# Two-block model on one core: shared modulation sums, index keys first, diagonal norms

## What is computed

```python
# first block
ada = c @ w_ada + b_ada                        # [1024] @ [1024, 6144]
shift1, scale1, gate1, shift2, scale2, gate2 = split(ada, 6)
h = rms_norm(x, g_norm1) * (1 + scale1) + shift1
zq, zk, zv, ziq, zik, ziw, zp, zg = split(h @ w_in)
q = rms_norm(zq by head, g_q); k = rms_norm(zk, g_k); ik = rms_norm(zik, g_ik)
# every query takes the 64 keys with the best index score:
#   sum over 4 index heads of relu(iq . ik) * iw, then softmax attention over them
y_attn = attention(q, k, zv, chosen) @ w_up_attn
y_pool = pool_mixer(zp) @ w_up_pool
g_attn, g_pool = split(sigmoid(zg))
x = x + gate1 * ((g_attn * y_attn + g_pool * y_pool) @ w_out)
h2 = rms_norm(x, g_norm2) * (1 + scale2) + shift2
x = x + gate2 * peer_ffn(h2)                   # 16384 experts, 8 heads, top 16
# second block: rms_norm, recurrent branch, sparse attention, w_out, rms_norm, gated FFN
```

## Time and profile before

| | |
|---|---|
| median of three runs | 1694.33 us |
| profiled execution, its own time | 1695.2 us |
| its span, first to last instruction | 1693.4 us |
| TensorE busy | 1560.6 us, 92% |
| VectorE, ScalarE, GpSimd busy | 1108.9, 841.4, 1102.9 us |
| mean granted TensorE clock | 0.968 of full speed |
| DMA | 280.07 MB, mean 165 GB/s |

### The profile page before, as it was taken

How to read it: one execution, slowest core, us unless ns; L and a number is a source line. 1 busy time by engine, 2 the same in 40 slices (tenths; PEclk the granted TensorE clock), 3 DMA queues, 4 the chain that set the end, 5 groups by cost and what they waited for, 6 DMA issues and landing times. The chain is left out here.

```text
span 1693.4 us, 27007 instructions
## 1 busy us (share of the span) xinstructions
PE 1560.6 (92%) x9679; PEld 1367.5 (81%) x9679; DVE 1108.9 (65%) x1674; ACT 841.4 (50%) x1432; POOL 1102.9 (65%) x453
## 2 busy tenths in 40 slices
PE   1789868999999999999999999999999988799999
PEld 1666536999999999988888888798877756699987
DVE  6555456799937777768888888761645364268760
ACT  1443304555556666645545454547654364454442
POOL 0663004688986666658888888856883622578896
PEclk9989889999999999999999999999999989999999
DMA  7645365455454444435555555535543511445554
GB/s 264 234 141 186 116 222 182 162 186 174 166 172 149 148 138 138 140 120 190 197 188 196 191 193 195 197 113 198 199 162 127 159 51 38 137 159 179 185 186 138
DMA packets 77397, 280.07 MB, mean 165 GB/s; under 512 B 8577, under 2 KB 9089, under 8 KB 77186
## 3 DMA queue, kind: packets, MB, share of 16 engines
q1 hardware_dynamic: 76592, 276.68, 48.3%
q10 hardware_dynamic: 722, 2.27, 0.4%
HBM read 277.86 MB, written 1.05 MB: 165 GB/s over the span
## 5 line engine op out<-in xcount | busy, mean ns | idle before, releaser
L1977 POOL TENSOR_TENSOR low<-ring,high 128x1024 fp32r<-128x1024 f32 x449 | 1102.6, 2468 | 579.9 <-ACT high L945 579.7
L945 ACT ACTIVATE high<-ring 128x1024 fp32r<-128x1024 f32 x449 | 472.2, 1057 | 419.6 <-PE PS L346 400.2
L344 PE MATMUL PS<-hTh,high 128*128 128x256 f32 (+1 forms) x1648 | 472.4, 287 | 7.3 <-POOL low L1977 6.1
L346 PE MATMUL PS<-hTh,low 128*128 128x256 f32 (+1 forms) x1648 | 467.7, 284 | 0.0
L345 PE MATMUL PS<-hTl,high 128*128 128x256 f32 (+1 forms) x1648 | 467.5, 284 | 0.0
L344 PE MATMUL PS<-high,hTh 128*128 128x512 f32 x940 | 371.9, 396 | 15.8 <-POOL low L1977 10.9
L345 PE MATMUL PS<-low,hTh 128*128 128x512 f32 x940 | 368.5, 392 | 0.0
L346 PE MATMUL PS<-high,hTl 128*128 128x512 f32 x940 | 368.4, 392 | 0.0
L1725 DVE TENSOR_TENSOR hTl<-region,hTh 128x256 fp32r<-128x256 f32 x128 | 289.1, 2260 | 59.8 <-ACT hTh L1177 59.8
L344 PEld LDWEIGHTS PS<-hTh,high 128*128 128x128 f32 (+1 forms) x1648 | 317.6, 193 | 10.2 <-POOL low L1977 5.4
L345 PEld LDWEIGHTS PS<-hTl,high 128*128 128x128 f32 (+1 forms) x1648 | 317.1, 192 | 0.0
(11 more groups left out here) (287 smaller groups left out, 1568.5 us busy)
## 6 DMA issues: line engine op xcount, KB each, us to landing
ring<-in_stream SPq DMA_DIRECT2D x523, 512.0 KB, 3.3
X<-in_x SPq DMA_DIRECT2D x1, 1024.0 KB, 5.0
region<-in_band ACTq DMA_DIRECT2D x1, 1024.0 KB
result<-X SPq DMA_DIRECT2D x4, 256.0 KB, 2.0
region<-in_skeys ACTq DMA_DIRECT2D x1, 512.0 KB
region<-in_consts ACTq DMA_DIRECT2D x1, 352.0 KB, 3.8
region<-in_wpool ACTq DMA_DIRECT2D x1, 256.0 KB
cols<-in_cols SPq DMA_DIRECT2D x1, 208.0 KB, 5.0
```

Of the source, the lines that this page charges most:

```text
L344: pe.matmul(out_, sh, mh, start=start, stop=False, **kw)
L346: return pe.matmul(out_, sl, mh, start=False, stop=stop, **kw)
L945: act.activation(high[:, b % RING, :], ring[:, b % RING, :], ACT.Copy).then_inc(rounded[b % RING], 1)
L1977: pool.tensor_tensor(low[:, b % RING, :], ring[:, b % RING, :], high[:, b % RING, :].bitcast(F32), ALU.subtract).then_inc(left[b % RING], 1)
```

## The change

1. **Modulation blocks 0 to 3 are shared.** TensorE multiplies quarters 0 and 2 itself (`ada_product`), into one row of PSUM, which ScalarE copies to `ada_row`; VectorE keeps quarters 1 and 3. The closing sums on TensorE are then four matmuls of the row and four with `ones`.
2. **n1's transposes come ahead of the modulation sums**, and ScalarE rounds two quarters of in0 before it splits n1. Five loads (band, wpool, brow, skeys, iota) are issued by ScalarE after the index keys and not before n1's split; lambda's work moves behind the attention.
3. **Index keys first.** Their squares, sum, root and scaling are done alone; TensorE transposes the index queries straight from `Z`, then the keys (six transposes) between in2 and in3. Queries and keys are scaled during in3 and transposed (ten) between the pooling products and in6, behind the copies of the pooling.
4. **Blocks 9 and 4** leave their places: `ada9` and `ada4` stand ahead of up_attn in the stream, and VectorE does one quarter of them in each of the eight steps of the attention loop. Sums 6 to 9 follow m1's transposes.
5. **up_attn and out1 finish bank by bank** (`bank_done`), VectorE gates each bank as it is done, and m1's first eight transposes start after three of them. Sums 4 and 5 stand after out1's second quarter instead of its third.
6. **Norms by a diagonal.** Rows are no longer scaled: VectorE writes diag(1/rms) for both token tiles, and the transpose becomes a float32 matmul of `X` with it. The root takes scale and bias itself.

```diff
-PAIRED = {"in1": "ada6", "in6": "ada7", "up_pool": "ada8", "up_attn": "ada9", "out0": "ada5", "out1": "ada10",
+PAIRED = {"in1": "ada6", "in6": "ada7", "up_pool": "ada8", "out0": "ada5", "out1": "ada10",
...
-    for name in [...] + ["up_pool", "up_attn", "ada4", "out0", "out1", "pq0", "pq1"]:
+    for name in [...] + ["up_pool", "ada9", "ada4", "up_attn", "out0", "out1", "pq0", "pq1"]:
...
+        ADA_ON_PE = (0, 2)
...
 # TensorE
-            def transposes(tag, src, ready, n_ready):
-                pe.wait_ge(sem(ready), n_ready)
+            def transposes(tag, src, ready, n_ready, by=None, first_half=None):
+                pe.wait_ge(sem(ready), first_half or n_ready)
                 for c in range(KC):
+                    if first_half and c == KC // 2:
+                        pe.wait_ge(sem(ready), n_ready)
                     for t in range(T):
...
+                        if by is None:
+                            last = pe.transpose(dst, part, ident[:, :])
+                        else:
+                            last = pe.matmul(dst, part, by[:, t, :], start=True, stop=True)
...
+                    if j < 4:
+                        for q in range(4):
+                            pe.matmul(PS[:, 7, 4 * j + q:4 * j + q + 1], ada_row[0:1, j, q * P:(q + 1) * P],
+                                      ones[0:1, 0:1], start=(q == 0), stop=False, skip_group_check=True)
+                        wait_used(pe, f"ada{j}")
...
+            def ada_product(j, q):
+                wait_loaded(pe, f"ada{j}", q)
+                for c in range(2):
+                    last = pe.matmul(PS[0:1, 5 + j % 2, :], col("cT", 2 * q + c), slot(f"ada{j}", q)[:, c, :],
+                                     start=(q == ADA_ON_PE[0] and c == 0), stop=(q == ADA_ON_PE[-1] and c == 1))
+                free_slot(f"ada{j}", q, last)
...
-            for j in range(4):
-                wait_used(pe, f"ada{j}")
-                ada(j)
-            transposes("n1", XN1, "norm_scaled", nth_norm("n1", T, T))
+            transposes("n1", X, "norm_scaled", nth_norm("n1", T, T), by=diag)
+            for j in range(5):
+                for q in ADA_ON_PE:
+                    if j < 4:
+                        if j >= 2 and q == ADA_ON_PE[0]:
+                            pe.wait_ge(sem("ada_row_kept"), j - 1)
+                        ada_product(j, q)
+                    if j and q == ADA_ON_PE[0]:
+                        pe.wait_ge(sem("ada_row_kept"), j)
+                        ada(j - 1)
...
-            transposes("qk1", N1, "qk1_normed", 1)
+            turned1(5, Z)
+            turned1(6, Z)
+            pe.wait_ge(sem("ik1_normed"), 1)
+            turned1(7, N1).then_inc(sem("ik1_turned"), 1)
             z1(3)
-            pe.wait_ge(sem("turned_kept"), kept_by("qk1", KC))
+            pe.wait_ge(sem("ik1_kept"), 2)
...
+            pe.wait_ge(sem("pool_kept"), 4)
+            pe.wait_ge(sem("qk1_normed"), 1)
+            for c in range(5):
+                last = turned1(c, N1)
+            last.then_inc(sem("qk1_turned"), 1)
             z1(6)
...
-            for j in (6, 7, 8):
-                wait_used(pe, f"ada{j}")
-                ada(j)
             attention("a1")
             pe.wait_ge(sem("attn1_kept"), 2)
+            token_major("up_attn", OT1, lambda t, o: 4 + 2 * t + o, per=1, inner=D, bank_done="up_done")
+            transposes("m1", M1, "m1_ready", 4, first_half=3)
+            for j in (6, 7, 8, 9):
+                wait_used(pe, f"ada{j}")
+                ada(j)
...
-            out1(0, 1, 2)
+            out1(0, 1)
             for j in (4, 5):
...
-            out1(3)
-            transposes("n2", XN1, "norm_scaled", nth_norm("n2", T, T))
+            out1(2, 3, done="out1_done")
+            transposes("n2", X, "norm_scaled", nth_norm("n2", T, T), by=diag)
...
 # VectorE
+                link(dve.reciprocal(tiny[:, 6:6 + T], tiny[:, 4:4 + T]))
+                for t in range(T):
+                    dve.tensor_tensor(diag[:, t, :], ident[:, :], tiny[:, 6 + t:7 + t].broadcast_to([P, P]),
+                                      ALU.mult).then_inc(sem("norm_scaled"), 1)
...
+                    if tag == "a1" and u < n:
+                        ada((9, 4)[u // QUARTERS], [u % QUARTERS])
...
+            normed1_heads(slice(9, 10), 1, [(896, IK1, 9, 1, 2)], "ik1_normed")
...
+            normed1_heads(slice(0, 9), 3, [(0, 0, 0, H1, 1), (512, K1, H1, 1, 2)], "qk1_normed")
...
-            ada(9)
-            ada(4)
-            wait_used(dve, "up_attn")
...
+                        dve.wait_ge(sem("up_done"), 2 * t + half + 1)
```

More of the change, by code:

```diff
@@ L94, in plan @@
     order = [f"ada{j}" for j in range(4)]
-    for name in [f"in{i}" for i in range(Z1B)] + ["up_pool", "up_attn", "ada4", "out0", "out1", "pq0", "pq1"]:
+    for name in [f"in{i}" for i in range(Z1B)] + ["up_pool", "ada9", "ada4", "up_attn", "out0", "out1", "pq0", "pq1"]:
         order += [name] + [PAIRED[n] for n in [name] if n in PAIRED]
@@ L666, in _, with out1 @@
             pe.wait_ge(sem("y_pool_kept"), 4)
[L667 removed]
+            pe.wait_ge(sem("qk1_kept"), 3)
+            attention("a1")
+            pe.wait_ge(sem("attn1_kept"), 2)
+            token_major("up_attn", OT1, lambda t, o: 4 + 2 * t + o, per=1, inner=D, bank_done="up_done")
+            transposes("m1", M1, "m1_ready", 4, first_half=3)
+            for j in (6, 7, 8, 9):
                 wait_used(pe, f"ada{j}")
                 ada(j)
[L670 to L676 removed]
             pe.wait_ge(sem("turned_kept"), kept_by("m1", KC))
+            def out1(*quarters, done=None):
+                token_major("out1", MT1, lambda t, o: 5 + 2 * t, quarters=quarters, bank_done=done)
+            token_major("out0", MT1, lambda t, o: 4 + 2 * t)
             pe.wait_ge(sem("ada_kept"), 2)
[L680 to L684 removed]
+            out1(0, 1)
             for j in (4, 5):
@@ L791, in _ @@
                         last.then_inc(sem("v_done"), 1)
[L794 removed]
+            transposes("n3", X, "norm_scaled", nth_norm("n3", T, T), by=diag)
             for i in range(RT_N):
@@ L1552, in _, with normed1_heads @@
-            dve.memset(m8[:, :], 0.0).then_inc(sem("qk1_normed"), 1)
-            keep_turned("qk1", NT1, lambda c: col("gain1", c))
+            def normed1_heads(heads, root, parts, done):
+                by_token = [st1[:, i, :].rearrange("p (t h) -> p t h", t=T)[:, :, heads] for i in range(3)]
+                dve.wait_ge(sem("qk1_root"), root)
+                link(dve.reciprocal(by_token[0], by_token[1]))
+                for t in range(T):
+                    for dst, src, h, n, dup in parts:
+                        weight = bc(st1[:, 0, 10 * t + h:10 * t + h + n], 2, HD)
+                        value = Z[:, t, src:src + n * HD].rearrange("p (h d) -> p h d", h=n)
+                        ins = dve.tensor_tensor(N1[:, t, dst:dst + dup * n * HD].rearrange("p (h d) -> p h d", h=dup * n),
+                                                value if dup == 1 else value.broadcast_to([P, dup, HD]),
+                                                weight if dup == 1 else weight.broadcast_to([P, dup, HD]), ALU.mult)
+                ins.then_inc(sem(done), 1)
@@ L1613, in _ @@
             for half in range(2):
-                wait_used(dve, f"out{half}")
                 for t in range(T):
+                    if half and not t:
+                        dve.wait_ge(sem("out1_done"), 1)
+                    else:
+                        wait_used(dve, f"out{half}")
                     o = half * NB
```

182 lines of the change are left out of this document (98 added, 84 removed).

## The result

The changed kernel takes 1678.31 us (median of three runs, 1677.88 to 1681.22) against 1694.33: a ratio of 0.9912, 95% interval 0.9889 to 0.9934. The profiled execution has a span of 1676.1 us against 1693.4, 17.3 less. Two later sets of runs of the same file, each beside the kernel before on the same chip, gave 1682.13 against 1696.37 and 1680.97 against 1697.80, a ratio of 0.9892 (0.9842 to 0.9943) and 0.9908 (0.9880 to 0.9935), with spans of 1684.2 and 1681.4.

What follows compares the result with a forecast made beforehand. TensorE was taken as the bound, busy 1560.6 of 1693.4 us, its idle 133 us nearly all there was to win. Terms summed to -13.0: 1695.2 to 1682.2, or 1681 against the median; range 1669 to 1692.

Steps and rivals of the forecast that it cites:

- Index keys first: Block 2 to block 3 of the projection: nearly all of TensorE's wait and slow transposes go, -10.3 us.
- rival 2: GpSimd's passes hold the new VectorE operations; index keys, then scoring, come 5 us late: 1686 us; chance 0.14.
- The ten other transposes: Behind the pooling copies: TensorE waits for ScalarE's four copies, 2.1 us, and transposes, 1.1: +3.2 us.
- Start: From the start to projection block 2: sums gain little, the first product follows them sooner; -6.5 us, bounds -9 and +8.
- Attention: Attention loop: eight modulation quarters added to VectorE only partly fit its idle time; +8.8 us with 1 for the clock.
- rival 4: Attention loop: the added quarters fill all of VectorE's idle time, +4 us instead of +8.8, total 1676; chance 0.12.
- up_attn to out0: Between these two products: sums gone from the path, gates bank by bank; -8.5 us after allowing for low clock.
- The end of out1: t=0's bank ends 3.4 us early and out0's gates no longer wait for gate1: -1.4 us.
- the prediction's last sentence: Wrong if the peer stage starts within 3 us of the old start, or a new wait behind it takes the gain.
- Norms by a diagonal: Three norms on the path: 16 more records each outweigh the scaling saved; +4.1 us, between 0 and +8.5.
- Rival 3: Diagonal for nothing: true matmuls lift the clock early, so the norms' price goes, 4.1 us less, 1677; chance 0.15.
- Rival 1: Low clock, slower: half clock stays in the four modulation blocks and the attention loop, total 1699 us; chance 0.09.

Runs made afterwards that it cites:

- c0: The changed kernel again, unchanged, timed beside the kernel before: 1682.13 us against 1696.37, ratio 0.9892.
- c1: The changed kernel once more, unchanged, timed beside the kernel before: 1680.97 us against 1697.80, ratio 0.9908.
- The two experiments on it: Each on the changed kernel: n2's squares ahead of ScalarE's roundings, 1677.48 us; out1's last two quarters not bank by bank, 1677.96 us.
- both orders: Changed kernel with block 0's products before n1's transposes, n2's squares before the roundings, and an earlier table load: 1665.54 us, later 1664.30.

## Why the prediction was right, and where it was not

The forecast of 1681 was 2.7 us above the result, and the two later medians, 1682.13 and 1680.97, lie within 1.2 us of it. The mechanism was right for the index keys, the ten transposes, the sums before attention and up_attn; the closeness of the sum is in part luck, as errors of 3 to 7 us in three terms cancelled. The steps:

- **Index keys first** came as worked out: no wait before block 3, transposes at full clock (0.82 us), -9.7 to -11.3 against -10.3. (The -9.7 of the first profile holds a fall of the clock inside block 2, 0.50 granted from 79.1 to 82.5; the other two have none there.) The two multiplies were held, 3.65 us together, but were done at 86.1, 4.5 us before TensorE came, so rival 2 fell:

```profile
82.49 3.65 DVE L1596 TENSOR_TENSOR region<-region 128x128 f32<-128x128 f32 x2
```

- **The ten other transposes** measured +3.1 for +3.2, 1.66 of it the wait for ScalarE's copies; **the sums before attention** -3.0 for -2.9. **Block 3** gave -0.9 for +0.5: scoring held nothing back, and the slow products that the forecast had counted with the index keys lay here, at 0.50 granted to 104.7 before.
- **Start** failed in size: -1.7 for -6.5. The failed step is the walk through the ring, "products 17 to 20" and "last sum at about 41.5". I let the transposes run from 10.8; they came at 12.48, since the diagonal needs ScalarE's root and its table load now stands behind the wait for eps (7.14 us). And I counted the slots as if loads went on meanwhile; the first reload left at 20.75. In between TensorE's clock once fell, to 0.50 granted:

```profile
34.70:38.10 3.40, 3.40 (x5) 0.47 (x5) 1.50 (x2) 0.00 (x0) 0.00 (x0) 0.50 0.79 304
```

  That is at most 1.7 us lost. In c0 there is no such fall and the last sum ends 1.2 us earlier; in c1 there are two and it ends 1.6 us later. The second half held roughly: the first product came 3.4 us after the last sum for 3.5 in the first profile, 5.2 and 4.3 in c0 and c1.
- **Attention** failed in size the other way: +4.7 to +5.6 for +8.8. The failed step is "eight quarters, each 1.54 us (L1494 x2), some 12 in all", set against "6.7 idle, of which about 4.7 lie where a quarter is issued". The windows over the whole stage, before and after, as in the earlier trace rows:

```profile
176.15:197.46 21.31, 19.04 (x122) 12.14 (x121) 13.29 (x34) 11.84 (x44) 0.00 (x0) 0.76 0.01 2
```

```profile
163.91:189.88 25.97, 21.66 (x120) 13.68 (x120) 23.41 (x50) 11.86 (x44) 0.00 (x0) 0.67 0.57 193
```

  VectorE's busy time grew by 10.1 us (10.8 in c0 and c1), not 12.4, and its idle time fell from 8.0 to 2.6: 5.5 us were filled (5.2), not 4.7. The result lies nearer rival 4's +4 than the forecast. The 1 us for the clock is not refuted: without the quarters (blocks 9 and 4 behind attention) the stage took 22.99 us at 0.70 granted, against 21.31 at 0.76 before.
- **up_attn to out0**: -8.9 to -10.7 for -8.5, with the parts as listed (products 14.0, half the transposes 1.1, sums 4.6). In c0 and c1 the products took 16.8 us, as the low clock ran on into up_attn; the forecast had +2 for that.
- **The end of out1** failed in its sign: -2.2 for that and the norm's shorter chain, measured +3.7 to +4.7. The step "t=0's bank ends 3.4 us early ... Only 1.4 of 2.8 us are left" looked at VectorE alone. What it left out is what is queued ahead of the squares on ScalarE, two roundings, and that their load needs the slot of out1's third quarter, which the bank-wise finish and the earlier sums 4 and 5 free only 1.5 us ahead of out1's end. This is the new wait behind the gain that the prediction's last sentence named as its danger; it took 6 to 7 us of it. The two experiments on it show the order and the bank-wise finish, the issue of the load the place of the sums.
- **Norms by a diagonal**: of +4.1 for three, about +1.7 (or -1.0 with n2's squares first) at n2, about 0 at n3 and about +1 at n4 are measured. At n3, from the end of the v loop to the next transposes that both kernels share, the scaled kernels took 160.2 to 160.5 us and the diagonal ones 157.6 to 161.8; from the end of the second block's output projection to the last instruction 215.9 to 216.0 and 215.9 to 217.5. The 16 records more lie in a stretch that runs at half clock anyway. Windows over the transposes and then the products behind them, with scaled rows, then with the diagonal (the kernel with n2's squares first):

```profile
1086.50:1089.80 3.30, 3.30 (x17) 3.30 (x17) 1.31 (x4) 2.15 (x6) 0.00 (x0) 0.50 0.00 0
1089.80:1092.00 2.20, 2.20 (x12) 2.20 (x11) 2.13 (x6) 2.19 (x5) 0.00 (x0) 0.51 0.00 0
```

```profile
1085.20:1091.70 6.50, 6.50 (x33) 6.50 (x34) 1.90 (x5) 2.52 (x6) 0.00 (x0) 0.56 0.00 0
1091.70:1094.00 2.30, 2.30 (x22) 2.30 (x21) 1.60 (x4) 2.21 (x4) 0.35 (x1) 1.00 0.00 0
```

  With scaled rows the products behind pay for the low clock, with the diagonal the transposes do. Rival 3 wanted the price at nothing; some 2.7 of 4.1 remain in the changed kernel, and about nothing only with n2's squares first. Its reason did not show: it wanted them done in under 5 us, and the 32 records took 5.2 to 6.8 everywhere behind n1 but for three traces at n3, with 3.84. The Trainium skill (TensorE: Matmul & The Clock Gate, Part 4) has transposes not counted as busy; by that rule true matmuls should have brought the full clock sooner. These traces don't show it: a mean of 0.56 over 6.5 us is some 5.7 us at half, and before, the transposes and products of n3 were at 0.50 for 5.3 us.
- **Rival 1**, the low clock, took at most 1.7 us at the start in the first profile, where its price was 14.8: the last sum ended at 46.5, not past 57. (Its price was summed too low: a last sum at 60 and 3.5 us to the first product make block 2 some 10 us late by the forecast's own figures, not 8.3.)

So errors cancelled: the start fell 4.5 to 5.5 us short, n2's wait cost 6 to 7 unforeseen and out0 with out1 1 to 2, while attention and up_attn gave 4 to 6 more than forecast. That leaves a sum of -9 to -12 like that of the two later traces. In the first profile a further 5.7 came behind the start of the u loop, where the others have 0.3 and 3.0. Part of that is n3 at the full clock (below), part the expert loops, and neither is the program: from the last transposes of the u loop to the end of the v loop the traces of all kernels take 352.6, 353.8 to 354.0 or 355.7 to 355.8 us, each with the same one wait of TensorE, 2.1 us, inside. The granted clock sorts them: it falls to 0.50 not once at the turn of the loops in the four short ones, once in the four middle ones and twice in the six long ones. The first window is of a short one (both orders), the second of a long one (c0):

```profile
720.00:724.00 4.00, 4.00 (x19) 3.30 (x19) 3.05 (x2) 1.40 (x3) 3.21 (x2) 1.00 0.07 25
```

```profile
740.00:744.00 4.00, 4.00 (x13) 3.11 (x12) 2.54 (x2) 0.81 (x2) 2.37 (x1) 0.60 0.00 0
```

13 products in 4 us against 19. What decides how often it falls there stays open.

## What to carry to other kernels

When two engines share the work on a ring that is refilled in order, the work on the oldest slot should go first: here two quarters' products put ahead of sixteen transposes were worth 7.5 us, and the sharing without it was worse than none by 5.9. When a product is finished bank by bank, or when work that stood between its quarters moves, ask when its last slots come free, and what stands on another engine's queue waiting for the loads that go there, ahead of the work that the early bank was to release. An engine's own rounding "ahead" is only free while its load is sure to be in.

## What the runs showed of the hardware

- The same 32 records at n3, in the same program and behind the same wait of 3.59 us, took 3.84 us at 1.00 granted in the first profile and 6.65 us at 0.54 in c0. So the program alone does not set the grant. Windows of the two:

```profile
1087.90:1091.40 3.50, 3.50 (x32) 3.50 (x33) 1.49 (x4) 2.27 (x6) 0.00 (x0) 1.00 0.00 0
```

```profile
1093.30:1099.70 6.40, 6.40 (x33) 6.40 (x33) 1.78 (x5) 2.52 (x6) 0.00 (x0) 0.54 0.00 0
```

- At the start the column of the granted clock shows 1.00 from 12.50 to 18.70 us, yet the 32 records there took 6.26 us (3.84 at the full level). To 17.6 us they start every 0.21 us, the last eight every 0.11. The durations, not the column, show the clock in the first microseconds.
- ScalarE's table load runs where its first user stands: behind a wait for eps it ran at 7.14 us in the changed kernel, and ahead of that wait the squares began at 7.09 instead of 8.54.
